# Experts of three prompt tiles computed over the whole expert table, the table read in chunks of 128 rows

## The reference, cut to what matters

```python
def one(xb):                                   # 128 tokens
    q = (xb @ w_pq).reshape(PEER_BLOCK, PEER_HEADS, 2, PEER_QDIM // 2)
    s = jnp.einsum('phcd,hckd->phck', q, sub_keys).astype(jnp.float32)
    ts, ti = lax.top_k(s, PEER_TOPK)
    cand = ts[:, :, 0, :, None] + ts[:, :, 1, None, :]
    cidx = ti[:, :, 0, :, None] * N_KEYS + ti[:, :, 1, None, :]
    fs, fpos = lax.top_k(cand.reshape(PEER_BLOCK, PEER_HEADS, -1), PEER_TOPK)
    eidx = jnp.take_along_axis(cidx.reshape(PEER_BLOCK, PEER_HEADS, -1), fpos, axis=-1)
    g = jax.nn.softmax(fs, axis=-1)
    u = u_tab[eidx]
    v = v_tab[eidx]
    a = jax.nn.gelu(jnp.einsum('pd,phkd->phk', xb, u).astype(jnp.float32), approximate=False)
    return jnp.einsum('phk,phkd->pd', (g * a).astype(v.dtype), v)
```

## Time and profile before

| | us |
|---|---|
| median of 2 runs | 2862.87 |
| the two runs | 2858.52 and 2867.22 |
| span of the profiled execution, first to last instruction | 2849.4 |
| TensorE busy | 1959.6 |
| VectorE busy | 1637.4 |
| ScalarE busy | 397.6 |
| GpSimd busy | 652.7 |

### The profile page before, as it was taken

How to read it: one execution, slowest core, us unless ns; L and a number is a source line. 1 busy time by engine, 2 the same in 40 slices (tenths; PEclk the granted TensorE clock), 3 DMA queues, 4 the chain that set the end, 5 groups by cost and what they waited for, 6 DMA issues and landing times.

```text
span 2849.4 us, 19084 instructions
## 1 busy us (share of the span) xinstructions
PE 1959.6 (69%) x6466; PEld 1073.8 (38%) x6466; DVE 1637.4 (57%) x3431; ACT 397.6 (14%) x993; POOL 652.7 (23%) x585
## 2 busy tenths in 40 slices
PE   7997789997786522677777776775666676852334
PEld 4433556695486411333233333332233232631110
DVE  3303733302369887565666666655765666477766
ACT  1101123211011100111111011101121111010010
POOL 0000000000000213343344343332433342232232
PEclk9998755556997766789889888997888887676677
DMA  3214160003000457899989999896988889885586
GB/s 109 89 74 34 5 212 1 1 1 158 34 1 1 173 207 321 363 382 363 372 345 357 378 373 360 329 372 261 365 345 317 339 330 403 351 354 236 236 332 266
DMA packets 114049, 680.20 MB, mean 239 GB/s; under 512 B 28768, under 2 KB 32544, under 8 KB 36448
## 3 DMA queue, kind: packets, MB, share of 16 engines
q0 software_dynamic: 83168, 604.55, 53.6%
q1 hardware_dynamic: 30784, 74.44, 8.1%
HBM read 672.55 MB, written 10.55 MB: 240 GB/s over the span
## 4 chain that ended last, share of the span: by engine, by line
PE 35%; DMA 21%; DVE 19%; POOL 7%; issue 5%; ACT 2%; POOLq 0%; DVEq 0%; ACTq 0%
PE bank L696 31%; DMA arena<-in_uv,arena 21%; POOL arena L677 7%; DVE arena L1635 4%; PE bank L708 3%; DVE arena L1430 3%; DVE arena L1427 2%; PE bank L1733 2%; DVE arena L1432 1%; ACT arena L1309 1%; DVE arena L1652 1%; DVE arena L1472 1%; DVE arena L1473 1%; DVE arena L1469 1%; ACT arena L1107 1%
## 5 line engine op out<-in xcount | busy, mean ns | idle before, releaser
L696 PE MATMUL bank<-arena 128*128 128x512 f32 (+13 forms) x4672 | 1513.1, 487 | 783.6 <-ACT arena L1309 658.4
L696 PEld LDWEIGHTS bank<-arena 128*128 128x128 f32 (+4 forms) x4672 | 809.4, 224 | 1423.3 <-ACT arena L1309 703.3
L677 POOL DMA_INDIRECT arena<-in_uv,arena x544 | 616.7, 1134 | 1671.2 <-PE bank L696 1537.7
L1635 DVE CUSTOM_DVE_ANT_0 arena<-arena 128x1024 f32<-128x1024 f32 x544 | 655.4, 1225 | 440.2 <-DMA arena<-in_uv,arena 436.5
L1652 DVE SCALAR_TENSOR_TENSOR arena<-arena 128x1024 f32<-128x1024 f32 x267 | 343.2, 1285 | 9.5
L1733 PE MATMUL bank<-arena 128*128 128x512 f32 (+13 forms) x972 | 312.0, 481 | 46.1 <-DVE arena L2086 15.3
L1733 PEld LDWEIGHTS bank<-arena 128*128 128x128 f32 (+3 forms) x972 | 157.9, 197 | 199.6 <-issue 160.9
L708 PE MATMUL bank<-arena 128*128 128x128 f32 (+3 forms) x716 | 141.5, 342 | 36.1 <-DVE arena L1395 11.8
L1304 ACT ACTIVATE arena<-arena 128x4 f32<-128x4 f32 x136 | 27.7, 204 | 881.6 <-DVE arena L1635 877.6
L1107 ACT ACTIVATE arena<-bank 128x512 f32<-128x512 f32 (+6 forms) x229 | 112.3, 517 | 231.4 <-PE bank L708 209.0
L708 PEld LDWEIGHTS bank<-arena 128*128 128x128 f32 (+3 forms) x716 | 97.2, 172 | 122.2 <-issue 73.5
(11 more groups left out here) (219 smaller groups left out, 683.4 us busy)
## 6 DMA issues: line engine op xcount, KB each, us to landing
arena<-in_w_pq SPq DMA_DIRECT2D x8, 2048.0 KB, 12.8
arena<-in_w_in SPq DMA_DIRECT2D x6, 2048.0 KB, 7.6
arena<-in_uv,arena POOLq DMA_INDIRECT x544, 11.0
arena<-in_w SPq DMA_DIRECT2D x4, 2048.0 KB, 13.8
arena<-in_w_out SPq DMA_DIRECT2D x4, 2048.0 KB
arena<-in_xT SPq DMA_DIRECT2D x1, 2176.0 KB, 8.5
arena<-in_C SPq DMA_DIRECT2D x1, 2064.0 KB, 10.3
out_s_C<-arena SPq DMA_DIRECT2D x1, 2064.0 KB
```

Of the source, the lines that this page charges most:

```text
L677: nc.gpsimd.indirect_dma_start(uv[r], None, i["uv"], bass.IndirectOffsetOnAxis(eidx_u[:, t, s0 + r:s0 + r + 1], 0))\
L696: return te.matmul(out, l, r, start=start, stop=stop)
L1635: last = ve.tensor_tensor_reduce(out=uv[r][:, 0:D], in0=uv[r][:, 0:D], in1=x_sb[:, t, :], scale=1.0, scalar=0.0, op0=ALU.mult, op1=ALU.add ...
```

## The change

Prompt tiles 1, 2 and 3 (`DENSE`) no longer gather their experts. For them the kernel goes over the whole table: for each chunk j of 128 experts it transposes u, multiplies it with h of all 384 tokens, takes the Gelu, multiplies by a dense matrix g[j] (128 experts x 384 tokens, mostly zero) of gate weights, and multiplies the result with v. Tile 0 and the samples gather as before, but in groups of 4 rows, all of them summed on DVE (the diagonal matrices on ACT and their matmuls on PE are gone).

The order is now: retrieve tile 1, build its g; the same for tiles 2 and 3; retrieve tile 0; then 24 groups of tile 0 with all pieces of the samples among them (K0 = 2, POOL issues block n in the same group as the piece that uses block n-2); then 128 chunks with the last 8 groups of tile 0 and the 8 groups of the samples among them; then the LayerNorms of tiles 1, 2, 3 and the samples.

Building g of a tile: PE transposes the 128 slots' i, j and weight, ACT copies them (`ijw`); DVE makes one-hot matrices for 8 tokens at a time (3 instructions of 128 x 1024); PE multiplies them per token (128 x 128 by 128 x 128) into a bank for 4 tokens; ACT copies the bank into `stage`, 8 MB, with the token as last index; SP writes `stage` to `g_rows` in DRAM in pieces of 512 B.

```diff
+DENSE = (1, 2, 3)
+ND = len(DENSE)
+TD = ND * P
+OB = 8
+        NC_, NP_ = 5, 4
+        uT = [pda.take(D).rearrange("p (c j) -> p c j", c=KC) for _ in range(2)]
+        P_ring = [pda.take(TD) for _ in range(NP_)]
+        g_ring = [pda.take(TD) for _ in range(NC_)]
+        c_ring = [pdb.take(2 * D) for _ in range(NC_)]
+        g_rows = nc.dram_tensor("g_rows", (NK, P, TD), F32, kind="Internal").ap()
-        K0, PER_STEP, PER_G = 7, 6, 11
+        K0, PER_STEP, PER_G = 2, 6, 11
+        GR = 4
+        N_G0, N_GS = SLOTS // GR, SLOTS // QB // GR
+        N_B = 24
+        N_C = N_G0 + N_GS - N_B
+        AFTER = [int((sum(WEIGHT[:k]) + WEIGHT[k] / 2) * N_B / sum(WEIGHT)) for k in range(N_PIECES)]
+        CYCLE, C_AT = 7, 3
# SP
-            sp.wait_ge(s_idx, PT)
+            for n in range(ND):
+                sp.wait_ge(s_gev, P // 4 * (n + 1))
+                sp.dma_start(g_rows[:, :, n * P:(n + 1) * P].rearrange("j i t -> i j t"), stage).then_inc(s_gw, 16)
+            sp.wait_ge(s_idx, 1)
...
+            sp.wait_ge(s_idx, 2)
+            sp.wait_ge(s_gw, 16 * ND)
+            for j in range(NK):
+                if j >= NC_:
+                    sp.wait_ge(s_yj, j - NC_ + 1)
+                sp.dma_start(c_ring[j % NC_], i["uv"][P * j:P * j + P, :]).then_inc(s_cl[j % NC_], 16)
+                sp.dma_start(g_ring[j % NC_], g_rows[j]).then_inc(s_cl[j % NC_], 16)
# POOL
-                j = AFTER[uses.get(n - 2, K0 - 2)] + 1
+                j = AFTER[uses.get(n - 2, K0 - 2)]
+            def group(g):
+                t, s0 = group_of(g)
+                for r in range(GR):
+                    if g >= 2 and r % 2 == 0:
+                        pool.wait_ge(s_vf, 2 * (g - 2) + r // 2 + 1)
+                    k = GR * (g % 2) + r
+                    nc.gpsimd.indirect_dma_start(uv[k], None, i["uv"], ...)
+            pool.wait_ge(s_idx, 1)
+            pool.wait_ge(s_gw, 16 * ND)
+            for g in range(N_G0):
+                group(g)
+                for n in sorted(issue.get(g, ())):
+                    load_chunk(n)
# PE: g of a tile
+                for b in range(P // 4):
...
+                    if b % (OB // 4) == 0:
+                        pe_eng.wait_ge(s_oh, bank // (OB // 4) + 1)
+                    if bank >= 2:
+                        pe_eng.wait_ge(s_gev, bank - 1)
+                    for k in range(4):
+                        at_k = b % (OB // 4) * 4 + k
+                        last = mm(PB[bank % 2][:, k * NK:(k + 1) * NK], ohi[z][:, at_k, :], ohj[z][:, at_k, :])
# PE: the chunks
+            def dots(j):
+                pe_eng.wait_ge(s_ue, 2 * (j + 1))
+                for c in range(KC):
+                    last = mm(PB[6 + j % 2][:, 0:TD], uT[j % 2][:, c, :], hTd[:, c, :], c == 0, c == KC - 1)
...
+                    if 3 <= c < 7:
+                        u_transpose(j + 1, c - 3)
+            def sums(j):
+                pe_eng.wait_ge(s_pm, j + 1)
+                for n in range(ND):
+                    for c2 in range(2):
+                        last = mm(PB[2 * n + c2][:, :], P_ring[j % NP_][:, n * P:(n + 1) * P],
+                                  c_ring[j % NC_][:, D + c2 * 512:D + c2 * 512 + 512], j == 0, j == NK - 1)
+                    if n == 0:
+                        for c in range(4, KC):
+                            u_transpose(j + 3, c)
+                last.then_inc(s_yj, 1)
+            for j in range(NK):
+                dots(j)
+                if j >= 2:
+                    sums(j - 2)
# ACT, in each chunk j: u_copy(j + 1, 0); Gelu of the dots, 128 x 384; u_copy(j + 1, 1)
# DVE: one-hots, 16 times a tile
+                    ve.tensor_tensor(ohi[z], io, slot_i, ALU.is_equal)
+                    link(ve.tensor_tensor(ohj[z], io, slot_j, ALU.is_equal))
+                    ve.tensor_tensor(ohj[z], ohj[z], slot_w, ALU.mult).then_inc(s_oh, 1)
# DVE: pieces and groups, then the chunks
+            for g in range(N_B):
+                dot_rows(g, range(GR))
+                for _ in range(pieces_at(g)):
+                    next(todo)
+                weigh_rows(g, range(GR))
+            for j in range(NK):
+                dve.wait_ge(s_cl[j % NC_], 32 * (j // NC_ + 1))
+                dve.wait_ge(s_pg, j + 1)
+                ve.tensor_tensor(P_ring[j % NP_], P_ring[j % NP_], g_ring[j % NC_], ALU.mult).then_inc(s_pm, 1)
```

More of the change, by code:

```diff
@@ new lines, in rest_tensor, with u_transpose @@
+            for _ in pieces():
+                pass
+            pe_eng.wait_ge(s_idx, 2)
+            for n, t in enumerate(DENSE):
+                fl = fill8(x_sb[:, t, :], P)
+            pe_eng.wait_ge(s_te, fl)
+            def u_transpose(j, c):
+                if j < NK:
+                    if c == 0:
+                        pe_eng.wait_ge(s_cl[j % NC_], 32 * (j // NC_ + 1))
+                        if j >= 2:
+                            pe_eng.wait_ge(s_pg, j - 1)
+                    if c == 4:
+                        pe_eng.wait_ge(s_ue, 2 * j + 1)
+                    last = tr(PB[6 + j % 2][:, c % 4 * P:(c % 4 + 1) * P], c_ring[j % NC_][:, c * P:(c + 1) * P])
+                    if c % 4 == 3:
+                        last.then_inc(s_up, 1)
@@ new lines, in rest_tensor @@
+            for c in range(KC):
+                u_transpose(0, c)
+            for j in range(NK):
+                dots(j)
+                if j >= 2:
+                    sums(j - 2)
+                else:
+                    for c in range(4, KC):
+                        u_transpose(j + 1, c)
+            sums(NK - 2)
+            sums(NK - 1)
+            pe_eng.wait_ge(s_vf, 2 * (N_G0 + N_GS))
+            pe_eng.wait_ge(s_pg, NK)
+            for c2 in range(2):
+                last = mm(PB[6 + c2][0:NS, :], C("ident4"), acc_v[:, c2 * 512:c2 * 512 + 512])
@@ L1311, in rest_scalar, with group_gelu @@
[L1311 to L1320 removed]
+            def group_gelu(g):
+                z = slice(GR * (g % 2), GR * (g % 2) + GR)
+                act.wait_ge(s_dot, g + 1)
+                sc.activation(gel[:, z], dots[:, z], ACT.Gelu).then_inc(s_gl, 1)
@@ new lines, in rest_scalar, with u_copy @@
+            todo = pieces()
+            for g in range(N_B):
+                group_gelu(g)
+                for _ in range(pieces_at(g)):
+                    next(todo)
+            for n in range(ND):
+                drain8(hTd[:, :, n * P:(n + 1) * P], P)
+            def u_copy(j, half):
+                if j < NK:
+                    act.wait_ge(s_up, 2 * j + half + 1)
+                    if j >= 2 and half == 0:
+                        act.wait_ge(s_ap, j - 1)
+                    sc.activation(uT[j % 2][:, 4 * half:4 * half + 4, :],
+                                  PB[6 + j % 2][:, :].rearrange("p (c j) -> p c j", c=4), ACT.Copy).then_inc(s_ue, 1)
@@ new lines, in rest_scalar @@
+            for half in range(2):
+                u_copy(0, half)
+            for j in range(NK):
+                u_copy(j + 1, 0)
+                act.wait_ge(s_ap, j + 1)
+                if j >= NP_:
+                    act.wait_ge(s_yj, j - NP_ + 1)
+                sc.activation(P_ring[j % NP_], PB[6 + j % 2][:, 0:TD], ACT.Gelu).then_inc(s_pg, 1)
+                u_copy(j + 1, 1)
+                g, k = group_at(j)
+                if g is not None and k == 2:
+                    group_gelu(g)
+                if g == N_G0 - 1 and k == 5:
+                    std(N_LAST0, P)
@@ L1322, in rest_vector @@
+            for n in range(ND):
+                std(N_LAST0 + 1 + n, P)
+            std(N_LASTS, NS)
         def rest_vector(dve, link, settle):
@@ L1628, in pieces @@
                 yield from retrieve(PT)
-            def dot_rows(j, half):
-                t = slots_of(j)[0]
-                for r in range(4 * half, 4 * half + 4):
-                    dve.wait_ge(s_uv[r], 16 * (j + 1))
-                    last = ve.tensor_tensor_reduce(out=uv[r][:, 0:D], in0=uv[r][:, 0:D], in1=x_sb[:, t, :],
-                                                   scale=1.0, scalar=0.0, op0=ALU.mult, op1=ALU.add,
-                                                   accum_out=dots[:, r:r + 1])
-                last.then_inc(s_dot, 1)
@@ new lines, in weigh_rows @@
+            def weigh_rows(g, rows):
+                t, s0 = group_of(g)
+                z = slice(GR * (g % 2), GR * (g % 2) + GR)
+                if 0 in rows:
+                    dve.wait_ge(s_gl, g + 1)
+                    link(ve.tensor_tensor(w8[:, z], gel[:, z], gw[:, t, s0:s0 + GR], ALU.mult))
+                for r in rows:
+                    k = GR * (g % 2) + r
+                    if s0 + r == 0:
+                        last = ve.tensor_scalar(acc_v, uv[k][:, D:2 * D], w8[:, k:k + 1], None, ALU.mult)
```

289 lines of the change are left out of this document (143 added, 146 removed).

## The result

The changed kernel takes 3528.28 us (two runs, 3526.84 and 3529.71), the kernel before 2862.87: a ratio of 1.233 (95% interval 1.2275 to 1.2391), 23% slower. The prediction was 3563 us with a range of 3400 to 3740.

The account below looks back on a forecast made before the run. It took DVE to bound building g, PE plus a serial knot the middle, and PE's matmuls the chunks: 1256 + 770 + 1494 + 30 = 3550 us of span, plus 13.5 around it, 3563 us; range 3400 to 3740.

Parts of the forecast that it names:

- Part 1: Until the first dense retrieval: +34 us, with DVE done with tile 1 at about 914 instead of 897.
- Part 2: Building three g, three retrievals and tile 0's: DVE sets 59 us a tile, g's write is hidden, end at 1256.
- Part 3: The loop with the samples' pieces: 770 us, bound by PE plus a serial knot; low end 660, high end 900.
- the knot: Middle loop: POOL's block waits hold up the next gathers, ACT's pieces stand behind Gelu; 21 us from piece to next dots.
- Part 4: The 128 chunks: 1494 us, PE-bound at 11.6 us each, with loads hidden and 36 weight loads a chunk counted at nothing.
- Part 5: The end: four LayerNorms one after the other and the last y, 30 us.
- Around the span: Outside the traced span: 13.5 us added to the 3550 us of span to reach the forecast time.
- Rival A: Middle loop: the knot is hidden, 660 us there and 3453 in all; chance 0.15.
- B: Building g: it is dearer, by its writes (+193) or ACT's strided copy (+54), 3620 to 3760 us; chance 0.12.
- C: Chunks: PE falls to the lower clock and they take twice the time, 5050 us; chance 0.03.
- D: Chunks: a dense float32 call costs one pass, not two; 6.3 us a chunk, 2885 us, no change; chance 0.02.
- E: Chunks: loads of 25 us are not hidden, leaving 5.5 us a chunk, 4270 us; chance 0.02.

Follow-up runs that it names:

- issue_later: The changed kernel with POOL issuing block n one group later, as the kernel before did: 3472.16 us.
- no_gathers: The changed kernel without the 24 groups of tile 0 among the samples' pieces, so tile 0 sums 32 of its 128 experts: 3382.76 us.
- ring4: The changed kernel with four slots for the chunks instead of five: 4161.99 us.
- best24_7: The changed kernel with bfloat16 dense products and g, blocks issued one group later, tile 0 retrieved first, seven chunk slots and three for P_ring: 2597.92 us.
- both_bf16: The changed kernel with bfloat16 operands in tiles 1 to 3's products of u with h and with v: 2795.12 us, ratio 0.975.

## Why the prediction was right

The likeliest case came true: the stages and what bounds each were as forecast. That the total came within 1% is in part luck, since the misses of parts 3 and 4 have opposite signs.

- **Part 1.** Tile 1 was retrieved at 918.9, for 914. The exponential waited for ACT's last score copy as forecast (DVE is idle for 17.49 us until it has run); the queries themselves stood 4.5 us later in this execution.
- **Part 2.** From the first one-hot of a tile to the end of its last it is 920.28 to 978.75, 58.5 us for 59. PE and ACT fit beneath: ACT's unknown strided copy took 1.06 us between the bounds of 0.60 and 2.4, 34 us a tile. Of the write of g, bounded at 23 and 123 us, 50 was taken; it took 30.4. At 276 GB/s it is near its lower bound, so the 120 ns a packet of the earlier trace rows were no price of a packet of 512 B. Nor did the floor of 42 us for SP's issue hold, priced from small pieces: the whole write took less. Tile 0's retrieval ended at 1261.3 for 1256.
- **Part 3.** 786 us for 770. The start took 26 for 28; compression 342.6 for 312; the rest 418 for 430, with 129 a group G for 132. Of the named mechanism, the knot, `issue_later` shows the POOL part, 56 us; the rest is argued. The term of a compression step was undersized, 43 for 39, though PE's share of it came out (36.3 for 36): two steps followed gave too little for what the groups bring. The low end, 660 with the knot hidden, was 639 in `no_gathers`, which has no groups; no order tried here reached it with the groups in. So here too two misses cancel: the pieces alone take 21 us less, and what the groups add is 147 us for the 110 between 660 and 770. (The terms of the tail, 89, 54 and 20, add up to 163 and not 165.)
- **Part 4.** About 1450 us for 1494, the largest miss: 0.325 and 0.43 us an instruction for 0.33 and 0.438, transposes at 0.11 between them. The chunk is 11.2 us for 11.6. That is a size and no mechanism: PE is busy for 1438.95 of 1442 us. The 36 weight loads were rightly counted at nothing: they are busy for 761.64 us of the same 1442, so nearly all of that lies beside matmuls, and 16 x 0.325, 12 x 0.43 and 8 x 0.11 us already fill the 11.2. The rule cited in part 4 from the Trainium skill (page "TensorE: Matmul & The Clock Gate", Part 3) would have made it 15.8; this trace disagrees as the one before did.
- **Part 5.** 29.9 us for 30.
- **Around the span.** 13.5 us were added. The run of 3529.71 us has the span of 3527.9, so 1.8 lie around it. The difference to the median of before was that of one execution to others: the 7 runs of it beside `ring4` spread over 16 us, each 1.8 over its own span. This term should have been 1.8. It and part 4 are too high, part 3 too low, and so 3563 stands 35 over 3528.

Rival A is refuted by the gaps of the middle; B by the write of 30.4 and the copy of 1.06 us (though in bfloat16 that copy became the bound, in `best24_7`); C by the clock of 1.00; D by two instructions a call, though `both_bf16`, 2.5% faster than the kernel before with calls of a quarter of the time, shows how much hung on this price (a call of half the time, D's case, was not run); E by the landing of 5 us, while `ring4` shows that with four slots it would have held.

## What to carry to other kernels

Before a gather is made dense, price the dense work on the engine that will do it, at its data type. Here three tiles cost PE 1430 us for 384 gathers that were worth 1114 us of DMA; at a quarter of the matmul time the same change is the basis of a version 10.7% faster. When a bound goes, look at the depth of the rings: here that was the next one (4, 5, 6 slots: 16.2 and 11.2 us a chunk in float32, 5.45 and 4.68 in bfloat16 with 5 and 6), so give the memory that the smaller type frees to slots. On an engine that issues in order, put no wait for a consumer's work between transfers that the same consumer needs next.

## What the runs showed of the hardware

- ACT's copy of 128 x 512 from PSUM: 0.60 us to contiguous float32, 1.06 with float32 values 512 B apart, 2.66 with bfloat16 values 256 B apart (2.31 from one to the next), and 0.60 with bfloat16 in runs of four values, read from PSUM with a stride of 512 B. Scattered single writes cost, strided reads did not.
- In `ring4`, with waits of 3.9 us on average in the chunks, the granted clock of 300 us fell to 0.91 from 1.00. Behind one wait of 2.9 us it stood at 1.00 until 3024 and at 0.51 from there to 3027, the lower level (1.2 GHz): pairs of instructions took 1.49 us instead of 0.81. So these waits cost more than their own length.
- The write of 8 MB to DRAM in pieces of 512 B took 30.4 us, and twice that for two. In `best24_7`, 4 MB in pieces of 256 B took 20.7 us: half the bytes in two thirds of the time.
- A product of 384 columns takes PE two instructions of 0.325 us in float32 and one of 0.16 us in bfloat16.
